# Opening an encoder layer with 128-row chunks of x: the first products split at token 256, the squares and the first cache loads later, the row of norms behind the second block

## The reference

```
u = rmsnorm(h) * g_mix_pre                     # h = x, per token over 1024 features
z = u @ w_in                                   # columns [A q | A k | A v | B q | B k | B v]
B heads: differential attention over z (8 heads, keys and values of 512 cached positions for the sample)
A heads: chunk-band attention over z (8 heads of 64)
...  gated merge, w_out, feed-forward with w_up / w_down, gate with w_ple     # not touched
```

## Time and profile before

| | |
|---|---|
| median of 3 runs | 1169.36 us |
| the profiled execution | 1171.4 us |
| its span, from the first to the last instruction | 1169.8 us |
| TensorE busy | 1142.7 us, 98% of the span |
| VectorE, ScalarE, POOL busy | 490.1, 426.2, 505.9 us |
| mean granted clock of TensorE | 0.993 |
| DMA | 98.82 MB, mean 84 GB/s |

### The profile page before, as it was taken

How to read it: one execution, slowest core, us unless ns; L and a number is a source line. 1 busy time by engine, 2 the same in 40 slices (tenths; PEclk the granted TensorE clock), 3 DMA queues, 4 the chain that set the end, 5 groups by cost and what they waited for, 6 DMA issues and landing times.

```text
span 1169.8 us, 23178 instructions
## 1 busy us (share of the span) xinstructions
PE 1142.7 (98%) x8356; PEld 1085.9 (93%) x8356; DVE 490.1 (42%) x926; ACT 426.2 (36%) x911; POOL 505.9 (43%) x420
## 2 busy tenths in 40 slices
PE   8999999999999999999999999999999999999898
PEld 7988888888888989999999899999999999999897
DVE  5665455565433341112441377215313421541655
ACT  6444444445444443232223353212212221232352
POOL 3436443454433333343446454544434444444641
PEclk9999999999999999999999899999999999999999
DMA  7224322232222222232222112322222222222122
GB/s 177 82 84 126 104 86 74 83 111 72 75 85 93 75 75 64 81 109 74 82 84 86 54 55 73 104 85 81 81 81 81 81 86 85 81 81 81 54 73 81
DMA packets 167370, 98.82 MB, mean 84 GB/s; under 512 B 8833, under 2 KB 162682, under 8 KB 167314
## 3 DMA queue, kind: packets, MB, share of 16 engines
q1 hardware_dynamic: 159570, 82.05, 24.4%
q0 software_dynamic: 7744, 16.02, 4.2%
HBM read 88.57 MB, written 11.02 MB: 85 GB/s over the span
## 4 chain that ended last, share of the span: by engine, by line
PE 90%; DVE 6%; ACT 1%; issue 1%; DMA 1%; SPq 0%; DVEq 0%; ACTq 0%
PE proj L1336 74%; PE turn_out L1537 3%; PE score L1455 3%; PE turn_out L1516 2%; PE turn_out L1532 1%; DVE wide L1202 1%; PE turn_out L1487 1%; PE score L1462 1%; DMA x_tm<-x_sample 1%; DVE hT L1231 1%; PE turn_out L1549 1%; DVE prob L1026 1%; ACT prob L676 1%; DVE act_lo L1220 1%; DVE act_lo L1224 1%
## 5 line engine op out<-in xcount | busy, mean ns | idle before, releaser
L469 POOL TENSOR_TENSOR w_lo<-w_raw,w_hi 128x512 fp32r<-128x512 f32 x292 | 393.6, 1351 | 592.7 <-ACT w_hi L624 592.4
L1336 PE MATMUL proj<-act_hi,w_hi 128*128 128x288 f32 x1568 | 353.9, 307 | 6.5 <-DVE act_lo L1224 3.4
L1336 PE MATMUL proj<-act_lo,w_hi 128*128 128x288 f32 x1568 | 336.6, 296 | 0.0
L1336 PE MATMUL proj<-act_hi,w_lo 128*128 128x288 f32 x1568 | 335.5, 296 | 0.0
L624 ACT ACTIVATE w_hi<-w_raw 128x512 fp32r<-128x512 f32 x292 | 182.4, 628 | 377.8 <-PE proj L1336 377.1
L1336 PEld LDWEIGHTS proj<-act_hi,w_hi 128*128 128x128 f32 x1568 | 249.3, 190 | 26.7 <-issue 16.6
L1336 PEld LDWEIGHTS proj<-act_lo,w_hi 128*128 128x128 f32 x1568 | 252.8, 189 | 0.0
L1336 PEld LDWEIGHTS proj<-act_hi,w_lo 128*128 128x128 f32 x1568 | 252.6, 189 | 0.0
L1336 PE MATMUL proj<-mid_hi,w_hi 128*128 128x288 f32 x640 | 137.4, 296 | 0.0
L1336 PE MATMUL proj<-mid_hi,w_lo 128*128 128x288 f32 x640 | 137.3, 295 | 0.0
L1336 PE MATMUL proj<-mid_lo,w_hi 128*128 128x288 f32 x640 | 137.3, 295 | 0.0
(11 more groups left out here) (211 smaller groups left out, 1149.9 us busy)
## 6 DMA issues: line engine op xcount, KB each, us to landing
w_raw<-w_in SPq DMA_DIRECT2D x72, 256.0 KB, 3.0
w_raw<-w_up SPq DMA_DIRECT2D x64, 256.0 KB, 2.8
w_raw<-w_down SPq DMA_DIRECT2D x64, 256.0 KB, 2.8
w_raw<-w_gate SPq DMA_DIRECT2D x32, 256.0 KB, 2.7
w_raw<-w_branch_b SPq DMA_DIRECT2D x16, 256.0 KB, 2.8
w_raw<-w_out SPq DMA_DIRECT2D x16, 256.0 KB, 2.8
w_raw<-w_ple_gate SPq DMA_DIRECT2D x16, 256.0 KB, 2.9
out<-k_tm POOLq DMA_DIRECT2D x12, 256.0 KB, 3.7
```

The costliest lines, as they stand in the source:

```text
L469: pool.tensor_tensor(w_lo[:, slot], w_raw[:, slot], w_hi[:, slot].bitcast(F32), ALU.subtract).then_inc(lo_done, 1)
L1336: last = pe.matmul(out[:, h], w[:, slot, at], x[:, k, HALF * h:HALF * h + HALF], start=(k == 0 and s == 0), stop=(k == blocks - 1 and s == 2))
```

## The change

x is loaded in five chunks of 128, 128, 128, 128 and 64 tokens, two before the first weight pieces and three behind. The two parts of the tokens are 0 to 255 and 256 to 575 (`X_PARTS`), so the tiles have 256 or 320 columns. The first two blocks of products use 256 columns of the one bank and 320 of the other; `vT` and `kT` are made from them by two VectorE instructions each. ScalarE squares chunk 0 ahead of the first tiles, 1 and 2 behind group 0, 3 behind group 1, 4 behind group 2. POOL issues the first cache loads behind the power, ahead of `lo_part(4)`. The other gains' transpose and the row come behind the second block of group 3, and the row is made by the helper that the later norms use (`row_matmuls`, line 1358). Sixteen products on zeros with half the rows become eight of 512 columns. The core of the diff:

```diff
-        XC, XR = 6, HALF // 3
-        ss_x, sq_x, r_x = small[0:XR, 0:XC], small[0:XR, 8:8 + XC], small[0:XR, 16:16 + XC]
+        ss_x, sq_x, r_x = small[:, 0:QB], small[:, 8:8 + QB], small[:, 16:16 + QB]
 
         with ExitStack() as start:
-            x_tm = sb("x_tm", [XR, XC, D], F32, start)
-            x_sq = sb("x_sq", [XR, XC // 3, D], F32, start)
+            x_tm = sb("x_tm", [P, QB, D], F32, start)
+            x_sq = sb("x_sq", [P, 2, D], F32, start)
...
+        X_PARTS = (slice(0, 2 * P), slice(2 * P, T))
+        X_CHUNKS = (range(0, 2), range(2, QB))
         X_TILES = [(GROUP * (g // 2) + j, g % 2) for g in range(4) for j in range(GROUP)]
...
-            for c in range(XC // 2):
-                sp.dma_start(x_tm[:, c], xp[XR * c:XR * c + XR]).then_inc(x_loaded[c], 16)
+            for t in range(2):
+                sp.dma_start(x_tm[:, t], xp[P * t:P * t + P]).then_inc(x_loaded[t], 16)
             for j in range(2):
                 piece(Count(j), k_half(w_in[0], 0, b_cols[j]))
-            for c in range(XC // 2, XC - 1):
-                sp.dma_start(x_tm[:, c], xp[XR * c:XR * c + XR]).then_inc(x_loaded[c], 16)
-            sp.dma_start(x_tm[0:XR - SMP, XC - 1], xp[SEQ - (XR - SMP):SEQ]).then_inc(x_loaded[XC - 1], 16)
-            sp.dma_start(x_tm[XR - SMP:XR, XC - 1], xs_d).then_inc(x_loaded[XC - 1], 16)
+            for t in range(2, QB - 1):
+                sp.dma_start(x_tm[:, t], xp[P * t:P * t + P]).then_inc(x_loaded[t], 16)
+            sp.dma_start(x_tm[0:SMP, QB - 1], xs_d).then_inc(x_loaded[QB - 1], 16)
...
+            pool.wait_ge(x_mean, 1)
+            pool.tensor_tensor(r_x[:, 0:QB - 1], sq_x[:, 0:QB - 1], neg_half[:, 0:QB - 1], ALU.pow)
+            pool.tensor_tensor(r_x[0:SMP, QB - 1:QB], sq_x[0:SMP, QB - 1:QB], neg_half[0:SMP, 0:1], ALU.pow
+                               ).then_inc(x_rooted, 1)
             pool.dma_start(ck[:, :].rearrange("p (j n) -> p j n", n=P),
                            cbk[:, 0:P].rearrange("(j p) n -> p j n", p=P)).then_inc(ck_loaded, 16)
             pool.dma_start(cv[:, :].rearrange("p (j n) -> p j n", n=P),
                            cbv[:, 0:P].rearrange("(j p) n -> p j n", p=P)).then_inc(cv_loaded, 16)
-            pool.wait_ge(x_mean, 1)
-            pool.tensor_tensor(r_x, sq_x, neg_half[0:XR, 0:1].broadcast_to([XR, XC]), ALU.pow).then_inc(x_rooted, 1)
...
             square_x(0)
-            square_x(1)
             act.wait_ge(gains_ready, 1)
             split_x(0)
             split_x(1)
             hi_part(Count(0))
             split_x(2)
+            split_x(3)
             hi_part(Count(1))
-            split_x(3)
+            square_x(1)
             square_x(2)
-            square_x(3)
             for i in range(4, 8):
                 split_x(i)
             hi_part(Count(2))
             hi_part(Count(3))
-            square_x(4)
+            square_x(3)
             for i in range(8, 12):
                 split_x(i)
-            square_x(5)
+            square_x(4)
...
-            for n in range(2):
-                projected(Count(0), n, pieces=3 + n)
+            for n, dst in ((0, vT[0]), (1, kT[0])):
+                dve.wait_ge(w_used, 3 + n)
+                for h, c in enumerate(X_PARTS):
+                    last = dve.tensor_tensor(dst[:, c], proj[n][:, 512 * h:512 * h + c.stop - c.start], x_row[:, c],
+                                             ALU.mult)
+                last.then_inc(proj_free[n], 1)
...
-            for c in range(3):
-                pe.wait_ge(x_loaded[c], 16)
+            for t in X_CHUNKS[0]:
+                pe.wait_ge(x_loaded[t], 16)
                 for i in range(GROUP):
-                    turn_x(i, (c,))
-                if c < 2:
-                    keep_warm(2, P)
-                else:
-                    keep_warm_halves(8, 512)
+                    turn_x(i, (t,))
+                keep_warm(*((2, P), (8, 512))[t])
...
-                        last = pe.matmul(acc[m][:, h], w[:, p, at], x[:, k, HALF * h:HALF * h + HALF],
+                        c = X_PARTS[h]
+                        last = pe.matmul(proj[m][:, 512 * h:512 * h + c.stop - c.start], w[:, p, at], x[:, k, c],
                                          start=(k == 0 and s == 0), stop=(k == KB - 1 and s == 2))
...
                 if group == 0:
-                    for c in range(3):
-                        pe.wait_ge(x_loaded[3 + c], 32 if c == 2 else 16)
+                    for t in X_CHUNKS[1]:
+                        pe.wait_ge(x_loaded[t], 16)
                         for i in range(GROUP):
-                            turn_x(GROUP + i, (c,))
-                if group == 3:
-                    pe.wait_ge(x_kept, 4 * GROUP)
-                    pe.wait_ge(rows_loaded, 16 * 5)
-                    pe.transpose(turn[:, 0:41], gain_rows[:, :], ident[0:41, 0:41]).then_inc(rows_turned, 1)
-                    pe.wait_ge(x_rooted, 1)
-                    for c in range(XC):
-                        at = 512 * (c // 3) + XR * (c % 3)
-                        last = pe.matmul(score[:, at:at + XR], r_x[:, c:c + 1].broadcast_to([XR, P]),
-                                         ident[0:XR, 0:XR], start=True, stop=True)
-                    last.then_inc(x_row_ready, 1)
+                            turn_x(GROUP + i, (t,))
                 for j in first_products(1, group):
                     if 0 < group < 3:
-                        turn_x(GROUP * (group + 1) + j, (0, 1, 2))
+                        turn_x(GROUP * (group + 1) + j, X_CHUNKS[(group + 1) % 2])
+            pe.wait_ge(x_kept, 4 * GROUP)
+            pe.wait_ge(rows_loaded, 16 * 5)
+            pe.transpose(turn[:, 0:41], gain_rows[:, :], ident[0:41, 0:41]).then_inc(rows_turned, 1)
+            pe.wait_ge(x_rooted, 1)
+            row_matmuls(r_x, rows).then_inc(x_row_ready, 1)
```

More of the change, by code:

```diff
@@ L262, in encoder_layer @@
         GROUP = KB // 2
+        X_PARTS = (slice(0, 2 * P), slice(2 * P, T))
+        X_CHUNKS = (range(0, 2), range(2, QB))
         X_TILES = [(GROUP * (g // 2) + j, g % 2) for g in range(4) for j in range(GROUP)]
         def x_bank(i):
-            return (score[:, 0:HALF], score[:, 512:512 + HALF],
-                    turn_out[:, 0:HALF], turn_out[:, 512:512 + HALF])[i % GROUP]
+            n = (2 * P, T - 2 * P)[X_TILES[i][1]]
+            return (score[:, 0:n], score[:, 512:512 + n], turn_out[:, 0:n], turn_out[:, 512:512 + n])[i % GROUP]
         acc = [p[:, :].rearrange("p (h n) -> p h n", h=2)[:, :, 0:HALF] for p in proj]
@@ L280, in encoder_layer @@
         proj_free = [sem(f"proj_free{b}") for b in range(2)]
-        x_loaded = [sem(f"x_loaded{c}") for c in range(XC)]
+        x_loaded = [sem(f"x_loaded{t}") for t in range(QB)]
         rows_loaded, lam_loaded, rel_loaded = sem("rows_loaded"), sem("lam_loaded"), sem("rel_loaded")
@@ L624, in hi_part, with square_x @@
                 act.activation(w_hi[:, slot], w_raw[:, slot], ACT.Copy).then_inc(hi_done, 1)
[L627 to L631, removed]
+            def square_x(t):
+                n = rows(t)
+                act.wait_ge(x_loaded[t], 16)
+                if t >= 2:
+                    act.wait_ge(x_squared, t - 1)
+                act.activation(x_sq[0:n, t % 2], x_tm[0:n, t], ACT.Square, accum_out=ss_x[0:n, t:t + 1]
                                ).then_inc(x_squared, 1)
@@ L636, in split_x @@
                 act.wait_ge(x_turned, i + 1)
-                act.activation(act_hi[:, j, HALF * h:HALF * h + HALF], x_bank(i), ACT.Copy,
+                act.activation(act_hi[:, j, X_PARTS[h]], x_bank(i), ACT.Copy,
                                scale=gcol[:, G_PRE + j:G_PRE + j + 1]).then_inc(g_hi, 1)
             square_x(0)
-            square_x(1)
             act.wait_ge(gains_ready, 1)
@@ L949, in _ @@
             for i, (j, h) in enumerate(X_TILES):
-                c = slice(HALF * h, HALF * h + HALF)
+                c = X_PARTS[h]
                 dve.wait_ge(g_hi, i + 1)
@@ L961, in _ @@
                 if i == 12:
-                    dve.wait_ge(x_squared, XC)
-                    dve.tensor_scalar(sq_x, ss_x, 1.0 / D, EPS, ALU.mult, ALU.add).then_inc(x_mean, 1)
+                    dve.wait_ge(x_squared, QB)
+                    dve.tensor_scalar(sq_x[:, 0:QB - 1], ss_x[:, 0:QB - 1], 1.0 / D, EPS, ALU.mult, ALU.add)
+                    dve.tensor_scalar(sq_x[0:SMP, QB - 1:QB], ss_x[0:SMP, QB - 1:QB], 1.0 / D, EPS, ALU.mult, ALU.add
+                                      ).then_inc(x_mean, 1)
             dve.wait_ge(rows_turned, 2)
@@ L970, in _ @@
             dve.wait_ge(x_row_ready, 1)
-            done(dve.tensor_copy(halves(x_row[:, :]),
-                                 score[:, :].rearrange("p (h n) -> p h n", h=2)[:, :, 0:HALF]))
+            done(dve.tensor_copy(x_row[:, :], score[:, 0:T]))
             settle()
@@ L1370, in keep_warm @@
                     pe.matmul(proj[1][:, 0:n], idle_w[:, :], idle_x[:, 0:n], start=True, stop=True)
```

(15 more changed lines are left out.)

## The result

The changed kernel takes 1177.22 us (median of 6 runs, 1174.03 to 1179.65); the kernel before, run beside it, 1170.74 (6 runs, 1168.92 to 1175.07): ratio 1.0052, 95% interval 1.0032 to 1.0071. Run again twelve times, beside 32 runs of the kernel before, it was 1177.26, ratio 1.0028 (1.0015 to 1.0041). So it is slower by about 0.3 to 0.5%; 1171.4 was forecast, at most 1176.

A forecast was written before the change was run, and what follows sets the result against it. TensorE, busy 98% of the span, was taken to bound the kernel. Loads 0, split +0.3, row +1.7 and cache loads 0 summed to +2.0 us, 1171.4 for the median; range 1168.5 to 1176.

The forecast's parts named there:

- The row's step: Before the third block: with the row behind the second block's products, nothing covers its copy and `vT`; +1.7 us.
- The wait on `vT`: Before the projection behind the second block: TensorE waits about 1.7 us for VectorE's `vT`, where 0.25 showed.
- The move of the cache loads: POOL's first cache loads behind the root: later root and `lo_part(4)` stay hidden; 0 us.
- The split: Opening loop, products split at token 256: groups 1 and 3 get longer, 2 shorter; +0.3 us by 28.46, bounds 0 to +0.5.
- the third block: The projection behind the first two blocks, 48 products: starts at 34.4 us for 32.46.
- The step on TensorE's columns: Opening loop, products split at token 256: columns are the same in sum, so TensorE's work is too.
- Whatever is late by then is late at the end: Behind 32.46 us the chain stays on TensorE, so the opening's delay carries unchanged to the end.
- rival 1: TensorE's clock falls in the new gap before the projection, losing 1.7 us more: +3.7, 1173.1 us; chance 0.22.
- The last x: Opening loads: x's last rows still land at 14.8 us, as many bytes lying before them; 0 us, bounds -1.6 to +2.0.
- The rate of 253 KiB/us: Opening loads: read from two stretches of the earlier trace and used to time the new chunks' landings.
- the first product: Opening: moves from 11.50 to about 11.0 us as the first weight piece comes earlier; gains nothing.
- rival 3: Clock falls between 12.4 and 14.8 us and stays low through the loop: +11, in all +13, 1182 us; chance 0.06.

The follow-up runs named there:

- both mends: Changed kernel with the row back between group 3's two blocks and the last chunk and row's last block over 128 rows: 1172.04 us, ratio 0.9999.
- full rows: Changed kernel with the last 64-row chunk's transposes and the row's last block taken over all 128 rows, 64 of them without tokens: 1174.62 us, ratio 1.0017.
- two clears: Changed kernel with two clears of unused columns added at the start of VectorE's program: 1174.35 us, ratio 1.0029.
- filled gap: Changed kernel with eight 512-column products on zeros put where TensorE would wait for `vT`: 1175.52 us, ratio 1.0025.
- only the row moved: Kernel before with the gains' transpose and its row of twelve products put behind the second block, everything else as before: 1175.36 us, ratio 1.0017.
- caches first: Changed kernel with POOL issuing the `ck` and `cv` loads ahead of the wait for the mean, as before: 1177.73 us, ratio 1.0039.
- before, three clears: Kernel before with three clears of one unused column each added at the start of VectorE's program: 1173.56 us, ratio 1.0023.
- both mended, clears on POOL: Changed kernel with the row between the blocks and 128-row operands, the two added clears on POOL instead of VectorE: 1173.93 us, ratio 1.0018.

## Why the prediction was wrong

**The opening was nearly right, in part by luck.** The row's step, forecast +1.7, is 1.67 and 1.62. The wait on `vT`, forecast about 1.7, is 1.71. The move of the cache loads is hidden, as forecast. The split was forecast at +0.3 up to group 3's last products: without the 64-row cost that stretch is 14.04 us for 13.64 (28.46 less 14.82 in the earlier trace rows), +0.40 and inside the bounds; a row of 1.26 us for 1.51 takes some of it back, so this opening as a whole is 17.91 for 17.64, 0.27. But that the third block, forecast at 34.4, starts at 34.22 is luck: TensorE took up the last x at 14.06 for 14.82, and from there it needed 20.16 us, 0.6 more than the forecast's 19.6.

**The step on TensorE's columns failed: it left out the rows.** "The columns are the same in sum, so TensorE's work is too" does not hold for the last chunk: in each of group 3's four tiles TensorE stands still at the change from 128 rows to 64 and back. The same mistake stands in the row, taken at 1.27 from the earlier trace rows; with a last block of 64 rows it took 1.56 by the same reading (30.99 to 32.55). Both together are 0.58 us, from both mends against the row moved back alone and again from full rows alone. The later norms' blocks in the earlier trace rows are all 128 rows ("128*128"), so the price could not be read there; the loads of `kT` had it.

**"Whatever is late by then is late at the end" is the step that failed by most.** It takes the rest of the kernel as given. But the change adds three VectorE instructions, and 1130 us later this makes the last stage 1.37 us longer (42.79 for 41.42). No row of the opening could have shown it.

**The clock behind the gap** was rival 1, at 0.22. The fall came in three of the six profiles with the gap (changed kernel twice, and with two clears), each time 1.4 to 1.5 us on the third block, and there in none of the seven without it. Yet the filled gap was no faster, and over all runs the clock takes the same from both kernels: span times one minus the granted clock is 9.9 us on average in the kernel before (32 runs) and 9.9 in the changed one (12). Every profile has other falls, as behind the waits at 661 and 1102 us in the earlier trace rows; why the mean comes out the same is not shown. So for the profiled execution the rival came true; for the median it is not shown to cost anything.

**The last x.** It was forecast unmoved, landing at 14.8. In the four profiles of kernels with 96-row chunks it lands at 13.78 to 14.78, mean 14.35; in the nine with 128 rows at 12.27 to 14.75, mean 13.59. That is 0.8 us sooner in the mean, with ranges that overlap. Behind it stand two errors that nearly cancel. The rate of 253 KiB/us, read from 96-row chunks, is too low for the new ones: the load that ends the first 2048 KiB (x and two weight pieces) is in at 9.31 to 10.79 us in the nine, at 11.31 to 11.86 in the four, and the first product, forecast at 11.0, starts at 9.82 to 10.37 for 11.28 to 11.80. The last 768 KiB then take 2.96 to 4.12 us for 2.47 to 2.92; why is not shown. So here too it is luck that the forecast came near. The Trainium skill's page "DMA: Bandwidth & Descriptors", section "Rules for kernel authors", wants 128 partitions in a transfer for the highest bandwidth. The direction agrees up to 10 us (398 to 418 GB/s from 7 to 10 us in the changed kernel, 239 to 309 in the kernel before); the chunks are larger as well, and no run here separates the two.

**The sum.** Taking the clock's share off every run, the mean of the changed kernel is 1166.8 us (12 runs) for 1163.0 (32), +3.8. The parts make 1.67 for the row, 0.27 for the split with the shorter row, 0.58 for 64 rows, 1.37 for the last stage: 3.9. By the same measure, each against the runs of the kernel before that stood beside it, and parts first, the others are:

| | parts | measured |
|---|---|---|
| row back between the blocks | 0.27 + 0.58 + 1.37 = 2.2 | 2.2 |
| only the row moved | 1.6 | 2.0 |
| full rows | 1.67 + 0.27 = 1.9 | 2.1 |
| gap filled | 3.9 + 0.17 = 4.1 | 4.1 |
| caches first | 3.9 | 4.2 |
| both mended | 0.3 | 1.1 |
| changed, two clears | 2.5 | 3.2 |
| before, three clears | 1.4 | 2.1 |
| both mended, clears on POOL | 1.6 | 3.0 |
| before, unchanged | 0 | 0.9 |

The order is right, and the kernel before against itself shows what the measure leaves open, 0.9 us; only the one with clears on POOL is clearly above its parts, by 1.4, which is not explained. The earlier x is in none of these sums. With its 0.8 us taken off, every row with 128-row chunks would be measured that much further above its parts, so either it does not count in the totals or another cost of that size hides it; this stays open.

So of the 3.8 us, 1.9 to 2.0 were the forecast, and 1.9 came from two costs that it did not have. The miss of 5.8 us in the median (1177.22 for 1171.4) holds those 1.9; 1.4 are the base, as the six runs of the kernel before give 1170.74 for the 1169.36 of three (its later sets 1172.58, 1172.95 and 1170.86); and 2.5 are in the first six runs alone: their difference of 6.5 us became 4.3 in the medians, 3.9 in the means, of the twelve and 32.

## What to carry to other kernels

Behind a chain of small products whose result frees the accumulator that the next big product needs, keep a block of independent products: moving them ahead of it cost their whole cover, 1.62 to 1.67 us for twelve products of 1.63 in the earlier trace rows. A short last chunk can cost more than a full one, where it takes TensorE's operands from 128 rows to 64 in the middle of a stream; chunks of 96 rows did not. And a gain or loss of 0.1% in a long kernel must be read from the profile's stages: three instructions more on an engine with time to spare moved another stage by 1.37 us.

## What the runs showed of the hardware

- At a change of TensorE's weight loads from 128 rows to 64 the engine stands still for 0.16 to 0.17 us in the streams read here, at a change to 96 rows not at all; three transposes with a last one of 64 rows take 0.62 us of TensorE, three with full rows 0.32, three with 96 rows 0.30.
- Three instructions more or less in VectorE's program move one operation's start by 0.36 us (0.46 after the one before it, for 0.10) in a stage 1130 us later, and with it which VectorE operation meets POOL's and takes 1.74 us for 0.76.
- The same program runs its projections of the gate in one of two steps, 6.24 or 6.40 us a block of 48 products, at a full clock; an execution keeps one of them throughout that stage of ten blocks.
- The low clock is not tied to the gap alone: with full rows it was at 0.57 from 15 to 19 us, in the loop, with TensorE busy all of that time but behind a wait of 1.29 us on the last x (busy 0.21 us from 14 to 15). The opening lost 1.7 us by it, well under the 11 us of rival 3, as it rose again by 19 us.
